# Two transformer-like blocks in one kernel: PSUM banks for intermediates, a different order of three openings, and attention 2 normalised at its output

## The chip, the cores and the metric

The kernel runs on one core of a Trainium2 chip. The metric is the device time of the whole kernel in microseconds (us). The engines work side by side and hand work over by semaphores: TensorE (PE) multiplies matrices into PSUM, VectorE (DVE) and ScalarE (ACT) compute elementwise and can read and write PSUM, GpSimd (POOL) computes elementwise on SBUF only, and SyncE (SP) issues the large transfers.

## The reference

The input is a sequence of 512 positions with 1024 channels, all in float32. The first block is run twice (two layers), the second block once.

```python
def first_block(x, ...):                         # two layers
    for l in range(2):
        h = rmsnorm(x, g_pre_mix[l])
        (c_q, c_kv, k_r, p_in, s_u, s_v, cv_b, cv_c, cv_x, gate_logits) = split_cols(h @ w_in[l])
        y_a = mla_branch(...) @ w_br_a[l]        # attention 1: 8 heads
        y_b = pool_branch(p_in, pool_w[l], pool_scale[l]) @ w_br_b[l]
        y_c = sgu_branch(s_u, s_v, ...) @ w_br_c[l]
        y_d = conv_branch(cv_b, cv_c, cv_x, ...) @ w_br_d[l]
        merged = sum(sigmoid(gate_logits)[b] * y for b, y in enumerate((y_a, y_b, y_c, y_d)))
        x = x + rmsnorm(merged @ w_out[l], g_post_mix[l])
        h = rmsnorm(x, g_pre_ffn[l])
        f = (silu(h @ w_ffn_gate[l]) * (h @ w_ffn_up[l])) @ w_ffn_down[l]
        x = x + rmsnorm(f, g_post_ffn[l])

def recurrent_block(x, ...):                     # the start of the second block
    gate, rec = split(x @ w_in)                  # 1024 channels each
    rec = causal_depthwise_conv(rec, conv_w, conv_b)           # 4 taps
    r, i = sigmoid(gates of rec)                 # 8 blocks of 128
    a = exp(-8 * r * softplus(-lam))
    h = scan(h = a * h + sqrt(1 - a * a) * (i * rec))          # along the sequence
    return (gelu(gate) * h) @ w_out

def second_block(x, ...):
    h = x + recurrent_block(rmsnorm_2(x, a_norm), ...)
    h = h + square(relu(rmsnorm_2(h, mlp_norm) @ w_up)) @ w_down
    k, v = shared_kv(h, ...)                     # keys normalised per head
    q = rmsnorm_2(rmsnorm_2(h, b_norm) @ w_q)
    p = softmax(q @ k.T * scale + bias)          # attention 2: 16 heads, chunk mask
    h = h + (p @ v) @ w_o
    return h + square(relu(rmsnorm_2(h, mlp_norm) @ w_up)) @ w_down
```

## The kernel before

Every tensor lies transposed: channels on the 128 partitions, the 512 positions along the row. X is 8 such tiles. A float32 product is made of three passes on rounded operands, `three` (matmuls at L831 to L833 for a whole unit): high part of the weights by high part of the data, high by low, low by high. The weights come in 476 **units** of 128 x 1024 words. A unit goes through four slots in SBUF: SyncE loads it (L309), ScalarE rounds it into the high part (`split_weights`, L370), GpSimd subtracts that into the low part in two halves (`low`, L340 and L342), TensorE multiplies it, 8 tiles by three passes, 24 products into one PSUM bank, and VectorE takes the bank. `tick(u)` on ScalarE splits unit u + 2. The data are split in the same way: a high part on ScalarE, a low part on VectorE (`x_lo` L1338, `lo_of` L1528).

Each engine has its instructions in an order written out by hand, and only semaphores tie them. Five places matter here.

- **The opening.** `norm` and `norm_tile` on ScalarE square a tile of X (L389) and make its high part (L391), tile by tile; VectorE (`norm_x`) adds the square to ACC (L1325) and makes the low part. TensorE runs the first unit tile by tile, then the sum of squares over the partitions (L901), then the second unit. ScalarE issues four small table loads before all that (L526).
- **The pool branch.** VectorE builds sums over windows of 2 to 16 positions from A (L1563 to L1574); TensorE multiplies them (L1088) right after unit 9 of the layer. Then come one unit, eight transposes for the gated branch (L1097), two units and its mixing (L1104). After the last input units and the value unit (L1119), attention 1 opens with scores (L1021).
- **The double norms**, four of them, where a block's output is normalised and added to X, and X at once normalised for the next block. VectorE copies or adds the last tile (L1373, L1657), ScalarE squares it and takes the root per position (L411), VectorE inverts it, ScalarE spreads it over 512 columns (RS2, L585), TensorE turns it (L913), and `post_norm` on VectorE scales, adds to X (L1357, L1358) and makes low parts. `together` on TensorE runs the first three units of the next block side by side, one tile of the data at a time, with a matmul for the sum of squares (L889) ahead of each tile.
- **The recurrent block.** ScalarE makes the first tap of the convolution (`tap`, L643), VectorE the other three (`conv`, L1692, L1693), TensorE the gates in four groups (`gates`), ScalarE sigmoids (L636, L637), tanh, exp, square and root, VectorE `gated`, `spread` (L1717), `recur` (L1723, L1724) and `product` (L1729). All intermediates are in SBUF. `together` starts the output units.
- **Attention 2**, 16 units of work of two heads and two blocks of queries. For each, TensorE computes scores (L946), VectorE adds the bias and takes maxima (`moved`, `maxima`, L1383 to L1392), ScalarE exponentiates (L440), VectorE inverts the sums (L1400), GpSimd scales the probabilities (L354), TensorE transposes them (L956), ScalarE copies them (L456 to L458), TensorE multiplies by the values (L969), ScalarE and VectorE split the output (L447, L1528).

## Time and profile before

| | us |
|---|---|
| median of 3 runs (2844.13 to 2852.17) | 2845.6 |
| the profiled execution | 2845.0 |
| its span | 2843.3 |
| TensorE busy in the span | 2737.2 (96%) |
| VectorE busy | 1229.2 (43%) |
| ScalarE busy | 1061.1 (37%) |
| GpSimd busy | 1340.3 (47%) |

The span is the time from the first to the last instruction in the profile; the execution's own time is 1.7 us longer. The busy shares are averages over the whole program. TensorE's mean granted clock was 0.982 of full speed; the profile knows two levels, 0.5 (1.2 GHz) and 1.0 (2.4 GHz). Matmul rows overlap, so the sum of their durations says more than the time they take one after the other.

### The profile page before, as it was taken

The numbers are of one execution on the slowest core, as the hardware profiler recorded it, in microseconds if no ns is written. First come the engines' busy times: TensorE is split into PE (matmuls) and PEld (weight loads), VectorE is DVE, ScalarE is ACT, GpSimd is POOL, SyncE is SP. The second block draws the span as 40 slices with busy tenths as digits, with TensorE's granted clock in tenths as the row PEclk, the third lists the DMA queues.
The fourth block names the chain that finished last, engine by engine and source line by source line (L and its number), as shares of the span: only waits on it lengthen the run. The fifth ranks groups of instructions, "written<-read, shape, count | busy, mean of one in ns | idle before, by whom it ended". The sixth has DMA issues, their size and how long they took to land.

```text
span 2843.3 us, 34289 instructions
## 1 busy us (share of the span) xinstructions
PE 2737.2 (96%) x12318; PEld 2213.5 (78%) x12318; DVE 1229.2 (43%) x1605; ACT 1061.1 (37%) x1566; POOL 1340.3 (47%) x1032
## 2 busy tenths in 40 slices
PE   8899999999999999999999999899999997899999
PEld 6688877888876888877888877688888885688887
DVE  5555555312246554455221268643224228453222
ACT  4244433322342344434222247433224347433222
POOL 4454543444453544453444445454444437454443
PEclk9999999999999999999999999999999998999999
DMA  3233332333332333322333322223333220123333
GB/s 132 82 97 97 104 87 69 97 97 98 98 100 74 104 95 98 97 89 74 97 97 96 97 89 82 81 90 97 98 97 126 80 88 8 52 91 98 97 99 97
DMA packets 72699, 259.15 MB, mean 91 GB/s; under 512 B 8192, under 2 KB 9088, under 8 KB 72448
## 3 DMA queue, kind: packets, MB, share of 16 engines
q1 hardware_dynamic: 71280, 254.17, 28.9%
q10 hardware_dynamic: 1296, 3.28, 0.3%
q8 instruction: 86, 1.41, 0.2%
q14 instruction: 37, 0.30, 0.0%
HBM read 255.31 MB, written 2.10 MB: 91 GB/s over the span
## 4 chain that ended last, share of the span: by engine, by line
issue 38%; PE 31%; POOL 26%; DVE 4%; ACT 1%; POOLq 0%; DVEq 0%
POOL w_lo L342 13%; POOL w_lo L340 12%; PE ps L831 9%; PE ps L833 9%; PE ps L832 9%; DVE XS L1808 1%; DVE fb L1807 1%; DVE st L1391 1%; POOL probs L354 1%; PE ps L1263 1%; PE ps L1265 1%; PE ps L1264 1%; ACT w_hi L370 0%; PE ps L1209 0%; ACT Y_hi L750 0%
## 5 line engine op out<-in xcount | busy, mean ns | idle before, releaser
L340 POOL TENSOR_TENSOR w_lo<-w_raw,w_hi 128x512 fp32r<-128x512 f32 x476 | 636.5, 1337 | 1466.0 <-ACT w_hi L370 1464.8
L831 PE MATMUL ps<-H_hi,w_hi 128*128 128x512 f32 x2240 | 901.8, 403 | 14.4 <-DVE H_lo L1338 13.8
L833 PE MATMUL ps<-H_hi,w_lo 128*128 128x512 f32 x2240 | 875.1, 391 | 0.0
L832 PE MATMUL ps<-H_lo,w_hi 128*128 128x512 f32 x2240 | 874.9, 391 | 0.0
L370 ACT ACTIVATE w_hi<-w_raw 128x1024 fp32r<-128x1024 f32 x476 | 500.0, 1054 | 583.9 <-DMA w_raw<-w_all 583.7
L342 POOL TENSOR_TENSOR w_lo<-w_raw,w_hi 128x512 fp32r<-128x512 f32 x476 | 654.4, 1375 | 0.0
L831 PEld LDWEIGHTS ps<-H_hi,w_hi 128*128 128x128 f32 x2240 | 422.8, 189 | 124.6 <-issue 24.9
L832 PEld LDWEIGHTS ps<-H_lo,w_hi 128*128 128x128 f32 x2240 | 422.9, 189 | 97.3 <-issue 12.5
L833 PEld LDWEIGHTS ps<-H_hi,w_lo 128*128 128x128 f32 x2240 | 422.1, 188 | 89.0
L831 PE MATMUL ps<-Y_hi,w_hi 128*128 128x512 f32 x1168 | 459.3, 393 | 19.5 <-POOL w_lo L342 11.5
L833 PE MATMUL ps<-Y_hi,w_lo 128*128 128x512 f32 x1168 | 456.5, 391 | 0.0
L832 PE MATMUL ps<-Y_lo,w_hi 128*128 128x512 f32 x1168 | 456.4, 391 | 0.0
L831 PEld LDWEIGHTS ps<-Y_hi,w_hi 128*128 128x128 f32 x1168 | 220.6, 189 | 67.4 <-POOL w_lo L342 12.4
L833 PEld LDWEIGHTS ps<-Y_hi,w_lo 128*128 128x128 f32 x1168 | 220.5, 189 | 46.6
L832 PEld LDWEIGHTS ps<-Y_lo,w_hi 128*128 128x128 f32 x1168 | 220.8, 189 | 45.3
L1807 DVE TENSOR_TENSOR fb<-fa,RS 128x512 f32<-128x512 f32 x64 | 63.4, 991 | 146.9 <-ACT fa L748 113.2
L1819 DVE TENSOR_TENSOR X<-X,ps 128x512 f32<-128x512 f32 x48 | 33.0, 688 | 207.5 <-PE ps L833 207.5
L1643 DVE TENSOR_TENSOR XS<-fb,ps 128x512 f32<-128x512 f32 x44 | 30.3, 688 | 194.7 <-PE ps L833 187.7
L606 ACT ACTIVATE Y_hi<-XS 128x512 fp32r<-128x512 f32 x44 | 27.8, 632 | 226.6 <-DVE XS L1645 226.6
L1454 DVE TENSOR_TENSOR G<-ps,RS 128x512 f32<-128x512 f32 x64 | 44.3, 692 | 135.0 <-PE ps L833 133.7
L474 ACT ACTIVATE G<-G 128x512 f32<-128x512 f32 x64 | 40.2, 631 | 157.3 <-DVE G L1454 157.3
L750 ACT ACTIVATE Y_hi<-XS 128x512 fp32r<-128x512 f32 x64 | 40.5, 632 | 141.2 <-DVE XS L1808 141.2
(240 smaller groups left out, 2513.0 us busy)
## 6 DMA issues: line engine op xcount, KB each, us to landing
w_raw<-w_all SPq DMA_DIRECT2D x476, 512.0 KB, 3.6
X<-xT SPq DMA_DIRECT2D x8, 256.0 KB, 6.5
rel_bias<-bias ACTq DMA_DIRECT2D x1, 2048.0 KB, 7.9
outT<-X SPq DMA_DIRECT2D x8, 256.0 KB, 3.4
sguw<-sgu_wT ACTq DMA_DIRECT2D x2, 256.0 KB, 4.4
sgub<-sgu_b ACTq DMA_DIRECT2D x2, 128.0 KB, 4.6
sgug<-sgu_g ACTq DMA_DIRECT2D x2, 128.0 KB, 5.1
CS<-cossin SPq DMA_DIRECT2D x1, 256.0 KB, 8.7
```

The source lines that it names most:

```text
L340: nc.gpsimd.tensor_tensor(w_lo[:, s, 0:UNIT // 2], w_raw[:, s, 0:UNIT // 2], f(w_hi[:, s, 0:UNIT // 2]), ALU.subtract).then_inc(w_lo_half, 1)
L342: nc.gpsimd.tensor_tensor(w_lo[:, s, UNIT // 2:UNIT], w_raw[:, s, UNIT // 2:UNIT], f(w_hi[:, s, UNIT // 2:UNIT]), ALU.subtract).then_inc(w ...
L370: nc.scalar.activation(w_hi[:, c % WSLOTS, :], w_raw[:, c % WSLOTS, :], ACT.Copy).then_inc(w_hi_ready, 1)
L474: nc.scalar.activation(dst, dst, ACT.Sigmoid).then_inc(sig_done, 1)
L750: nc.scalar.activation(Y_hi[:, j, :], XS[:, j % 2, :], ACT.Copy).then_inc(hi_ready, 1)
L831: MM(out, wh, xh, start=start, stop=False)
L832: MM(out, wh, xl, start=False, stop=False)
L833: return MM(out, wl, xh, start=False, stop=stop)
L1454: VE.tensor_tensor(dst, ps[:, bank(o), :], RS[:], ALU.mult).then_inc(g_lin, 1)
L1643: lk(VE.tensor_tensor(XS[:, j % 2, :], fb[:, j % 2, :], ps[:, (u0 + 2 * j + 1) % 4, :], ALU.mult))
L1807: lk(VE.tensor_tensor(fb[:, 0, :], fa[:, j % 2, :], RS[:], ALU.mult))
L1819: VE.tensor_tensor(X[:, m, :], X[:, m, :], ps[:, c % 4, :], ALU.add).then_inc(unit_out, 1)
```

## The change

- **Opening, layer 0.** ScalarE makes all eight high parts first, then the second unit's weights, then the squares; VectorE makes the eight low parts, then adds. TensorE runs units 0 and 1 before the sum of squares. The table loads of layer 0 are issued after the squares.
- **Pool branch, both layers.** The eight transposes and units 10 and 11 come ahead of the pool products; pool banks 4, 7, 7, 4. Input units 14 and 15 come ahead of the value unit, and the first scores wait for one unit less.
- **Double norms.** The last square of the mixing block is read from PSUM, ahead of the copy. The root's table is loaded by a dummy instruction. RS2 is no longer written: TensorE multiplies the 128 x 1 inverses, broadcast, by the identity. VectorE's second scaled tile comes between the add and the low part, ScalarE makes a tile's high part ahead of its square, and TensorE takes the sum of squares behind the tile's products. The merge before the first norm orders ScalarE's splits differently.
- **Recurrent block.** Taps 0 to 3, the squares, roots and drives of tiles 4 to 7 and all products go to PSUM banks 4 to 7. ScalarE's first sigmoids go ahead of tap 5, the split of the third output unit ahead of gelu 6. `together` begins the output units with two of them (`late=1`).
- **Attention 2.** GpSimd no longer scales the probabilities. TensorE turns the inverses with four more products per unit, ScalarE's third copy is 512 columns wide instead of 256, VectorE scales the output into XS, ScalarE makes its high part from there and GpSimd the low part.

```diff
-POOL_BANK = (4, 5, 6, 4)
-QK0, UV1 = 14, 16
+POOL_BANK = (4, 7, 7, 4)
+QK0, UV1 = 14, 17
+        def tapped(k):
+            return ps[:, 4 + k, :] if k < 4 else rec[:, k, :]
+        def spare(n):
+            return ps[:, 4 + n % 4, :]
+        def root_of(n):
+            return spare(n) if n >= 4 else lru_t[:, n, :]
...
             for h in range(H2):                                   # GpSimd, attention 2
-                g = 2 * H1 + h
-                eng.wait_ge(inv_ready, h + 1)
-                for n in range(4):
-                    o = kept(h, n // 2, n % 2)
-                    i = nc.gpsimd.tensor_scalar(o, o, st[:, g % 2, 12 + n:13 + n], None, ALU.mult)
-                i.then_inc(p_ready, 1)
+                eng.wait_ge(hi_ready, SPLIT["att2"] + h + 1)
+                nc.gpsimd.tensor_tensor(of_tiles(Y_lo, h // 2, h), scaled2(h), f(of_tiles(Y_hi, h // 2, h)), ALU.subtract).then_inc(lo_ready, 1)
...
                 if on_pe:                                         # ScalarE, norm_tile
+                    nc.scalar.activation(dst(k), src(k), ACT.Copy, scale=v(name, k)).then_inc(hi_ready, 1)
                     if k >= 2:
                         act.wait_ge(sq_summed, pb // 8 * 7 + k - 1)
...
-                    act.wait_ge(post_inv, p + 1)
-                    nc.scalar.activation(RS2[:].rearrange("p (j d) -> p j d", d=P), st[:, 0, 8:12, None].to_broadcast([P, 4, P]), ACT.Copy).then_inc(post_row, 1)
+                    nc.scalar.activation(hn[:, 0, 0:1], ones[:, 0:1], ACT.Sqrt)
...
+                    for k in range(DT):                           # ScalarE, opening
+                        act.wait_ge(x_loaded[k], 16)
+                        nc.scalar.activation(H_hi[:, k, :], X[:, k, :], ACT.Copy, scale=v("pre_mix0", k)).then_inc(hi_ready, 1)
+                    split_weights(1, 1)
...
+            gates(0)                                              # ScalarE, recurrent block
             tap(5)
-            gates(0)
...
+            tick(UAO)
             gelu(6)
-            tick(UAO)
...
                 for k in range(wide):                             # TensorE, together
                     tile(k)
-                    for u in range(u0, u0 + n):
+                    for u in range(u0, u0 + n - (1 if k < late else 0)):
+                        if late and k == late and u == u0 + n - 1:
+                            pe.wait_ge(w_lo_ready, u0 + n)
+                            for q in range(late):
+                                product(u, q)
                         product(u, k)
+                    if squares:
+                        squares(k)
...
-                pe.wait_ge(post_row, p + 1)                       # TensorE, post_norm
+                pe.wait_ge(post_inv, p + 1)
                 for j in range(4):
-                    m = nc.tensor.transpose(ps[:, 6, j * P:(j + 1) * P], RS2[:, j * P:(j + 1) * P], ident[:])
+                    m = MM(ps[:, 6, j * P:(j + 1) * P], st[:, 0, 8 + j:9 + j].to_broadcast([P, P]), ident[:], start=True, stop=True)
...
+                for s in (1, 0):                                  # TensorE, turn_pair
+                    for e in range(2):
+                        k = 12 + 2 * s + e
+                        m = MM(ps[64 * e:64 * e + 64, 6, (3 - s) * P:(4 - s) * P], st[:, u % 2, k:k + 1].to_broadcast([P, 64]), ident[:], start=True, stop=True)
...
-                    pe.wait_ge(p_ready, g + 1)
+                    pe.wait_ge(inv_ready, u + 1)
...
-                    lo_of("att2", h, of_tiles(Y_lo, h // 2, h), attended2, of_tiles(Y_hi, h // 2, h))   # VectorE
+                    VE.tensor_tensor(XS[:, h % 2, 0:2 * P], ps[:, 7, 0:2 * P], probsT2[:, h % 2, 10 * P:12 * P], ALU.mult).then_inc(scaled_done, 1)
```

On TensorE, around the pool branch of layer 0, the order before was this (SA and SB hold the window sums, A the input units' results, vnT the gated branch's normalised input):

```order
L831 MATMUL ps<-H_hi,w_hi 128x512 [waits unit_out,w_lo_ready]
...
L1088 MATMUL ps<-SA,poolw 64x512 [waits br_vec,layer_loaded]
L1088 MATMUL ps<-SB,poolw 64x512
...
L831 MATMUL ps<-H_hi,w_hi 128x512 [waits unit_out,w_lo_ready]
...
L1097 MATMUL ps<-ident,A 128x128 [waits unit_out,lo_ready]
L1097 MATMUL ps<-ident,A 128x128 x7
...
L1104 MATMUL ps<-sguw,vnT 64x128 [waits br_vec]
```

and now it is this:

```order
L1112 MATMUL ps<-ident,A 128x128 [waits unit_out]
L1112 MATMUL ps<-ident,A 128x128 x7
L844 MATMUL ps<-H_hi,w_hi 128x512 [waits unit_out,w_lo_ready]
...
L1121 MATMUL ps<-SA,poolw 64x512 [waits std_ready,br_vec,layer_loaded]
L1121 MATMUL ps<-SB,poolw 64x512 x2
L1121 MATMUL ps<-SA,poolw 64x512
...
L1128 MATMUL ps<-sguw,vnT 64x128 [waits br_vec]
```

The pool products moved behind the transposes and two units (48 products).

On ScalarE, in the recurrent block, from the split of the unit B2 + 8 on, the order before was this (Y_hi is a high part, rec the convolution, lru_r and lru_i the sigmoids):

```order
L626 ACTIVATE Y_hi<-rec 128x512 [waits src_ready] x2
L643 ACTIVATE rec<-recp,V 128x512 [waits unit_out]
L636 ACT_TABLE_LOAD
L636 ACTIVATE lru_r<-ps,V 128x512 [waits lru_mm]
L637 ACTIVATE lru_i<-ps,V 128x512
...
L370 ACTIVATE w_hi<-w_raw 128x1024 [waits w_loaded3]
```

and now it is this:

```order
L641 ACTIVATE Y_hi<-rec 128x512 [waits src_ready] x2
L651 ACT_TABLE_LOAD
L651 ACTIVATE lru_r<-ps,V 128x512 [waits lru_mm]
L652 ACTIVATE lru_i<-ps,V 128x512
...
L658 ACTIVATE rec<-recp,V 128x512 [waits unit_out]
L379 ACTIVATE w_hi<-w_raw 128x1024 [waits w_loaded3]
```

The tap of tile 5 moved behind the first four sigmoids.

On TensorE, one unit of attention 2 before (probs are the probabilities, probsT their transposes):

```order
L946 MATMUL ps<-K_59,Q_58 128x384 [waits s_free]
L946 MATMUL ps<-K_59,Q_58 128x384
L946 MATMUL ps<-K_59,Q_58 128x256 x2
L956 MATMUL ps<-ident,probs_55 128x128 [waits pt_a,p_ready]
L956 MATMUL ps<-ident,probs_55 128x128 x9
L969 MATMUL ps<-probsT_56,V_87 64x256 [waits lo_ready,pt_a]
```

and now:

```order
L965 MATMUL ps<-K_59,Q_58 128x384 [waits s_free]
L965 MATMUL ps<-K_59,Q_58 128x384
L965 MATMUL ps<-K_59,Q_58 128x256 x2
L975 MATMUL ps<-ident,probs_55 128x128 [waits pt_a,inv_ready]
L975 MATMUL ps<-ident,probs_55 128x128 x9
L980 MATMUL ps<-ident,st 64x128 x4
L992 MATMUL ps<-probsT_56,V_87 64x256 [waits scaled_done,pt_a]
```

The transposes wait for VectorE's inverse (inv_ready) and no longer for GpSimd (p_ready), and four products are new.

## Rows read from the trace of the kernel before

**Rows 1.** The page, part 1: busy us (share of the span) xinstructions
```profile
PE 2737.2 (96%) x12318; PEld 2213.5 (78%) x12318; DVE 1229.2 (43%) x1605; ACT 1061.1 (37%) x1566; POOL 1340.3 (47%) x1032
```

**Rows 2.** Waits of TensorE: who waited for whom, us in total, times, longest
```profile
PE ps L956 <- POOL probs L354: 14.6, 12, 2.9
PE ps L1088 <- DVEq L1576: 14.0, 2, 7.0
PE ps L831 <- DVE H_lo L1338: 13.8, 5, 10.9
PE ps L831 <- POOL w_lo L342: 11.5, 2, 10.8
PE ps L889 <- ACT SQ L385: 9.5, 4, 2.4
PE ps L909 <- DVE ACC L1325: 9.2, 4, 2.3
...
PE ps L913 <- ACT RS L585: 6.4, 4, 1.6
PE ps L831 <- issue: 5.8, 2, 5.5
```

**Rows 3.** Five stretches: length, busy PE PEld DVE ACT POOL, PE's clock, DMA share, GB/s
```profile
76.50:87.60 11.10, 4.08 (x10) 1.28 (x10) 8.23 (x12) 0.32 (x1) 0.71 (x1) 0.69 0.16 47
1726.00:1733.00 7.00, 5.39 (x13) 4.26 (x14) 6.00 (x8) 3.78 (x6) 3.33 (x2) 0.51 0.00 0
1790.90:1804.50 13.60, 5.60 (x13) 4.43 (x14) 12.44 (x16) 5.41 (x10) 3.39 (x2) 0.50 0.02 7
2364.30:2428.60 64.30, 51.62 (x395) 35.65 (x394) 56.29 (x103) 50.75 (x156) 59.85 (x56) 0.92 0.00 1
2428.60:2445.50 16.90, 12.75 (x86) 8.98 (x87) 1.60 (x5) 6.94 (x20) 8.54 (x8) 0.72 0.00 1
```

**Rows 4.** The opening in order of time: start us, us, instruction, idle before
```profile
10.94 0.77 PE L831 MATMUL ps<-H_hi,w_hi 128*128 128x512 f32 x1 [10.94 <-DVE H_lo L1338]
...
13.07 0.75 DVE L1338 SCALAR_TENSOR_TENSOR H_lo<-X,V,H_hi 128x512 fp32r<-128x512 f32 x1
...
20.63 1.64 DVE L1338 SCALAR_TENSOR_TENSOR H_lo<-X,V,H_hi 128x512 fp32r<-128x512 f32 x1
...
24.32 1.41 PE L831 MATMUL ps<-H_hi,w_hi 128*128 128x512 f32 x1
```

**Rows 5.** The first pool product of layer 0, in order of time
```profile
83.56 1.08 PE L1088 MATMUL ps<-SA,poolw 64*64 64x512 f32 x1 [7.02 <-DVEq L1576]
```

**Rows 6.** The double norm after layer 0's mixing block, in order of time
```profile
456.67 0.69 DVE L1373 COPY Dn<-ps 128x512 f32<-128x512 f32 x1 [3.18 <-PE ps L833]
...
460.86 0.63 ACT L585 ACTIVATE RS<-st 128x512 f32<-128x512 f32 x1 [0.31 <-DVE st L1353]
...
466.60 0.92 PE L831 MATMUL ps<-H_hi,w_hi 128*128 128x512 f32 x1
```

**Rows 7.** Groups of VectorE from 1696 to 1788: busy us, mean ns, idle before
```profile
L1692 DVE SCALAR_TENSOR_TENSOR rec<-recp,V,rec 128x512 f32<-128x512 f32 x16 | 17.8, 1111 | 1.8 <-ACT rec L643 1.3
L1717 DVE SCALAR_TENSOR_TENSOR lru_t<-lru_u,lru_t 128x512 f32<-128x512 f32 x8 | 9.8, 1226 | 0.4
```

**Rows 8.** The recurrent block's output units, in order of time
```profile
1794.34 1.04 ACT L370 ACTIVATE w_hi<-w_raw 128x1024 fp32r<-128x1024 f32 x1
...
1798.90 0.79 PE L831 MATMUL ps<-Y_hi,w_hi 128*128 128x512 f32 x1 [10.84 <-POOL w_lo L342]
```

**Rows 9.** Groups of attention 2, 2364.3 to 2428.6
```profile
L354 POOL TENSOR_SCALAR probs<-probs,st 128x384 f32<-128x384 f32 (+3 forms) x52 | 55.5, 1089 | 5.0 <-DVE st L1400 5.0
```

**Rows 10.** Attention 2, first copies of three of VectorE's units, in order of time
```profile
2364.29 0.42 DVE L1383 COPY probs<-ps 128x256 f32<-128x256 f32 x1 [0.63 <-PE ps L946]
...
2395.71 0.42 DVE L1383 COPY probs<-ps 128x256 f32<-128x256 f32 x1 [0.95 <-PE ps L946]
...
2424.18 0.42 DVE L1383 COPY probs<-ps 128x256 f32<-128x256 f32 x1
```

More of the change, by code:

```diff
@@ L848, in unit, with together @@
                 m.then_inc(w_used, 1)
-            def together(u0, n, xh, xl, ready, squares, wide=5):
-                pe.wait_ge(w_lo_ready, u0 + n)
+            def together(u0, n, xh, xl, ready, squares, wide=5, late=0):
+                pe.wait_ge(w_lo_ready, u0 + n - (1 if late else 0))
                 pe.wait_ge(unit_out, u0 + n - 4)
@@ L870, in together @@
                         m = product(u, k)
+                        if u == u0 and squares:
+                            squares(k)
                     m.then_inc(w_used, 1)
@@ L1082, in _ @@
                 gemm(w0 + 7, 3, Hh, Hl)
-                pe.wait_ge(layer_loaded, 64 * (l + 1))
-                pe.wait_ge(br_vec, 3 * l + 1)
-                for g in range(4):
-                    r = slice(64 * (g % 2), 64 * (g % 2) + 64)
-                    m = MM(ps[r, POOL_BANK[g], :], poolw[r, g // 2, :], (SA, SB)[g % 2][r, g // 2, 16:528], start=True, stop=True)
-                m.then_inc(br_mm, 1)
-                gemm(w0 + 10, 1, Hh, Hl)
-                pe.wait_ge(lo_ready, SPLIT[f"pool{l}"] + 2)
                 pe.wait_ge(unit_out, w0 + 8)
@@ L1098, in _ @@
                 m.then_inc(br_mm, 1)
-                gemm(w0 + 11, 2, Hh, Hl)
+                gemm(w0 + 10, 2, Hh, Hl)
+                pe.wait_ge(layer_loaded, 64 * (l + 1))
+                pe.wait_ge(br_vec, 3 * l + 1)
+                pe.wait_ge(std_ready, NORMS[f"ckv{l}"][0] + 1)
+                for g in (0, 1, 3, 2):
+                    r = slice(64 * (g % 2), 64 * (g % 2) + 64)
+                    m = MM(ps[r, POOL_BANK[g], :], poolw[r, g // 2, :], (SA, SB)[g % 2][r, g // 2, 16:528], start=True, stop=True)
+                m.then_inc(br_mm, 1)
+                gemm(w0 + 12, 1, Hh, Hl)
                 pe.wait_ge(br_vec, 3 * l + 3)
@@ L1183, in _ @@
                 gelu_unit(n)
-            together(UAO, 3, Yh, Yl, SPLIT["lru"], None)
+            together(UAO, 3, Yh, Yl, SPLIT["lru"], None, late=1)
             gemm(UAO + 3, DT - 3, Yh, Yl)
@@ L1345, in norm_x @@
                 for k in range(DT):
+                    x_lo(split, name, k)
+                for k in range(DT):
                     add_squares(name, k)
-                    x_lo(split, name, k)
                 link(root(name, RS[:]))
@@ L1581, in _ @@
                 dve.wait_ge(br_vec, 3 * l + 2)
+                take(10)
+                dve.wait_ge(a_chain, 5 * l + 5)
+                link(VE.reciprocal(st[:, 0, 12:16], st[:, 1, 8:12]))
+                for n in range(4):
+                    i = VE.scalar_tensor_tensor(vnT[:, n, :], ps[:, 5 + n // 2, (n % 2) * 256:(n % 2) * 256 + 256], st[:, 0, 12 + n:13 + n],
+                                                sgug[:], ALU.mult, ALU.mult)
+                    if n < 3:
+                        link(i)
+                i.then_inc(br_vec, 1)
+                dve.wait_ge(br_vec, 3 * l + 3)
+                take(11)
                 for t in range(2):
@@ L1615, in _ @@
                 project(l, w0 + QK0, N_PART * l + 1, 0)
-                take(14)
+                take(14, 15)
                 dve.wait_ge(w_used, w0 + UV1 + 1)
@@ L1621, in _ @@
                     freed(i_ == 3)
-                take(15)
                 for h in range(H1):
@@ L1625, in _ @@
                 attended(l)
-                for k in range(U_OUT):
+                for k in range(U_OUT - 1):
                     copy_out(U["out"] + k, Dn[:, k, :])
```

166 lines of the change are left out of this document (83 added, 83 removed).

## The prediction

> **What bounds the kernel now.** I read the page first, then the waits of TensorE, then seven stretches of the busy-time table, and only then rows in order of time. TensorE is busy 96% of the 2843.3 us span [rows 1]. So nothing that merely shortens work on ScalarE, VectorE or GpSimd counts; what counts is the time in which TensorE waits, and the time after a wait in which its products run at half clock. The list of its waits is short: the eight largest sum to 14.6 + 14.0 + 13.8 + 11.5 + 9.5 + 9.2 + 6.4 + 5.8 = 84.8 us, of which 10.9 is the start of the program [rows 2, 4]. The second loss is the clock. From 1790.9 to 1804.5 the granted clock is 0.50 (1.2 GHz of 2.4), and 13 products take 5.60 us, 0.43 each; at full clock that is 0.215, and a unit of 24 products about 5.3 us [rows 3]. So each microsecond of products at half clock loses half of itself. The change touches the place behind each of the eight waits. The sum is made against the profiled execution's 2845.0 us (span plus 1.7 around it); the median of the runs is 0.6 above it.
>
> **Opening.** Before, ScalarE squares and splits each tile of X in turn and VectorE adds a square between two low parts, so the first unit is fed one tile per 1.5 us: it starts at 10.94 and the second unit at 24.32 [rows 4]. That is 13.4 us for one unit and one sum. After, the eight high parts come first, one per 0.6 us, the squares behind them, and four table loads leave the head of ScalarE's queue. With TensorE at half clock for its first 12 products (5.2 us) and then at full clock (2.7), the unit takes 8 us from a start that is up to 1 us earlier. What hides the squares is the second unit (5.3 us), which now runs ahead of the sum. Eight adds at 0.7 to 1.0 us need 5.6 to 8, so I leave 1.3 us for a late sum. Gain 7 (bounds 4.5 and 9, the latter with no wait for the sum). A low part that runs beside GpSimd costs 1.64 us [rows 4], and the second unit's weights are now split beside the low parts; that is in the lower bound.
>
> **Pool branch and first attention slot.** The branch's four products wait 7.02 us for VectorE's window sums, once per layer: the 14.0 of [rows 2, 5]. After, TensorE first does the gate branch's eight transposes and two units (0.6 + 10.6 us), whose inputs were taken long before, and comes to the pool products at about 88 where the sums end at 83.5 [rows 5]. So 4.5 us of slack cover them, also if GpSimd's splitting slows the last sums. Gain 14.0. In the stretch after the wait the clock averages 0.69 [rows 3]; about 4 us of products at half clock there and 2.8 in the second layer give back 3.4. The value unit, moved behind the last input unit, lets the first scores wait for a unit whose copy is long done; that wait is 0.8 per layer, outside the eight. VectorE's four value copies then come ahead of the first maxima, under 16 us of gate products. Gain 19 (bounds 14 and 20).
>
> **The four double norms.** From the last product to the first of the next block there are 10.0 us: the copy that follows the last product begins at 456.67, ScalarE writes the row from 460.86 (0.63), products resume at 466.60 [rows 6]. After a mixing block the last square reads PSUM (-0.7), the weight split is moved ahead, the ScalarE hop of 0.63 with its two hand-overs goes (-0.9), and the high part comes before the square and the second add after the first low part (-0.7 each): 7.6. After an FFN the first saving is absent: 8.3. But the first sum of squares, some 0.9 us, was hidden in the old wait and now stands among the products, and products that begin sooner find the clock still low for longer. Net 0.6 per norm, 2.5 in all (bounds -3 and 8). The merge before the first norm, where the order of ScalarE's splits changes, I take at 1.5 (bounds -1 and 4).
>
> **Recurrent block.** Three waits: 0.7, 5.5 ("issue") and 10.8 (the 11.5 and 5.8 of [rows 2]). What stands behind them is VectorE. Its three-operand steps on SBUF average 1.11 us in the convolutions and 1.23 in the spreads [rows 7]; one beside an idle GpSimd takes 0.75, one beside a busy one 1.64 [rows 4]. An operand in PSUM leaves that conflict: four convolutions (12 steps), four spreads and four drives, 20 steps at 0.36 to 0.48 saved, 8 us on VectorE's chain. In the first part this brings the fourth and fifth convolution forward by some 5 us. ScalarE then does the first sigmoids ahead of tap 5, so that TensorE's second gate group no longer waits: 5.5 and 0.7 go, and of the 5.39 us of products at clock 0.51 [rows 3] half, 2.7; these 8.9 are not added, since the output unit below is where they count. What is late next is ScalarE: its second sigmoids stand behind tap 6, which waits for VectorE, and come about 5.5 us earlier, not 9; the fourth gate group then waits some 3.8 us where it waited 0.3. The large wait ends with the low half of the third output unit's weights, split at 1794.34 [rows 8] behind gelu 6. Now it is ahead of gelu 6, and two units begin with their first tile without it. Everything there follows the chain, 5.5 us earlier and shorter by the PSUM steps: I get the first output tile at about 1782 and the last of the 72 products at about 1800, where before it was at 1817 (start 1798.90 [rows 8], 72 x 0.215 = 15.5 of products, 2.8 of them twice for half clock [rows 3]). That is 17; 1.5 off for a new low stretch of clock behind the 3.8. Gain 15.5 (bounds 6, where the fourth group and the output unit wait as long as before less the order gain, and 20).
>
> The Trainium skill ("VectorE: DVE Perf Modes", the errata section) gives VectorE an operand from PSUM a larger fixed cost than one from SBUF, 120 cycles against 58. At its 0.96 GHz that is 0.065 us a step, and by the page 20 steps would lose 1.3 us. The trace does not bear it out: the SBUF step alone takes 0.75 [rows 4], the PSUM copy 0.69 [rows 6] (different operations, so only the nearest pair). The skill's "SBUF — State Buffer" (who interferes with whom) says that a VectorE step with two SBUF inputs and a GpSimd step block each other for the whole instruction. By that a contended step should cost up to its own 0.75 plus GpSimd's 1.3; the row shows 1.64 [rows 4], so the gain a step would be 1.3 by the rule and is 0.9 by the row.
>
> **Attention 2.** GpSimd scales the probabilities, 1.09 us a step and four a unit [rows 9], before TensorE may transpose them: 14.6 us of waits [rows 2]. After, transposes wait only for VectorE's reciprocal; the row is turned with four small products, and VectorE scales the 256 output columns. Where does the bound go? VectorE is busy 56.29 of 64.3 us [rows 3] and back to back between the two weight splits on GpSimd. Twelve units take 59.9 us, from 2364.29 to 2424.18, 4.99 each [rows 10]; the one that starts at 2395.71 waits for TensorE, which waits for GpSimd behind a weight split. Without those the units run at 4.5, and that is VectorE's own work, since scaling 256 columns out of PSUM takes what the low part took (0.42 by the copy of that size [rows 10]). So the steady part gains only 12 x 0.5 = 6. TensorE's busy 51.62 us [rows 3] are 4.0 a unit, partly at half clock; four more products at 0.13 (51.62 over 395) make 4.5, some 4.2 at full clock, against 4.5: close, and hidden while the clock is full. ScalarE's wider third copy adds 0.2 to 3.8. At the end the last three units are paced by GpSimd's 4.3 before, 16.9 us for 86 products at clock 0.72 [rows 3]; after, by transposes, copies and values, about 3.4. That is 4.5 more. GpSimd's low parts (0.7) hide behind the output unit's first seven tiles. Gain 9.5 of 10.5, for hand-overs (bounds 3 and 12).
>
> **Sum.** 7 + 19 + 2.5 + 1.5 + 15.5 + 9.5 = 55; 2845.0 - 55 = 2790.0, and about 2790 as a median too.
>
> **Rivals.**
> (a) Only the order gains come through. The recurrent chain through ScalarE holds TensorE up as before at the fourth gate group and the output unit (gain 6, not 15.5), or attention 2 gives 3 because VectorE, TensorE and ScalarE all stand within 0.5 us of the period: 2845 - 55 + 9.5 = 2799.5, or 2796.5; both, 2806. For it: VectorE is busy 88% of attention's body, and the last four convolutions stay in SBUF. Against: the low-part wait named GpSimd, whose place in the order has changed.
> (b) More comes: the opening's sum is in time, the norms' clock recovers at the same distance, the output unit is fed without a stall: 7 + 2 + 5 + 4.5 more, some 10 to 15 of it together, 2776 to 2780.
> (c) Waits only change place (the change does not do what it says): each moved wait reappears at the next hand-over, within 0.3%. Against it: the 7 us of the pool wait have two units with inputs long ready to fill them.
> (d) Slower: TensorE in attention 2 stays at 1.2 GHz. A unit there would cost it twice 4.2 = 8.4 us in place of 4.99, over 16 units 55 us lost in place of 9.5 gained: 2845 - 45.5 + 55 = 2854.5. It decides once products at half clock (8.4) outlast VectorE's period (4.5), so that TensorE never idles but never is granted full clock. For it: clock 0.72 in the tail and 0.92 in the body [rows 3]; against it: the body's clock rises in the stretches with fewer waits.
>
> **Chances.** Forecast (2784 to 2796) 0.50; (a) 0.29; (b) 0.15; (c) 0.02; (d) 0.02; 0.02 for something unseen. The likeliest is 2790. The range takes in (b) but for its end and (a) with both parts: 2775 to 2808, which leaves out about 2 in 10. 0.3% (8.5 us) is about what a measurement of this kernel can tell from no change: faster 0.95, same 0.025, slower 0.025.
>
> **What would show it.** No wait for the pool products, in either layer. Second unit at about 18 and the first sum after it. About 7.6 and 8.3 us between last and first product at the norms. No 5.5 us wait at the second gate group, a new one of some 4 at the fourth, and output units beginning near 1800 less what is gained before. In attention 2, copies 4.5 us apart throughout and a tail of about 12 us. Mean clock above the present one. It is wrong if TensorE's waits still sum to over 60 us, if VectorE's steps with PSUM operands take more than 0.8, or if the clock in attention 2 is below 0.85.

## The result and the profile after

| us | before | changed |
|---|---|---|
| median | 2848.9 (2844.1 to 2853.1, 4 runs) | 2808.7 (2807.1 to 2810.4, 4 runs) |
| the profiled execution's span | 2843.3 | 2808.7 |

The ratio is 0.9859 with a 95% interval of 0.9839 to 0.9880: the change makes the kernel 1.2 to 1.6% faster, 34 to 46 us. The forecast was 2790 with a range of 2775 to 2808. The direction was right, the gain too large, and the time lies just outside the range. Over all comparisons below the kernel before took 2840.9 to 2855.2; its profiled execution was one of the short ones (median 2851.7 in 17 runs), so against it the gain is smaller: 2843.3 - 2808.7 = 34.6 us of span where 55 were forecast. By medians it is 40.2 of 55. The forecast took 55 off the short execution's 2845.0; about 4 us of the 19 by which 2790 was missed are that base, and the other 15 are the terms.

Part 1 of the page of the changed kernel answers to [rows 1]. GpSimd has 48 instructions and 61 us less, TensorE 144 records more and 1.2 us less:

```profile
PE 2736.0 (97%) x12462; PEld 2220.7 (79%) x12462; DVE 1224.8 (44%) x1605; ACT 1064.9 (38%) x1566; POOL 1279.6 (46%) x984
```

These are its waits of TensorE, to be read beside [rows 2] (who waited for whom, us in total, times, longest):

```profile
PE ps L844 <- POOL w_lo L355: 17.6, 4, 10.7
PE ps L844 <- DVE H_lo L1361: 13.9, 5, 3.3
PE ps L928 <- DVE ACC L1348: 11.5, 4, 4.3
PE ps L975 <- ACT probsT L468: 7.2, 9, 1.5
PE ps L965 <- DVE probs L1411: 5.1, 3, 2.4
PE ps L844 <- issue: 3.5, 2, 3.3
PE ps L844 <- DVE M_lo L1540: 3.2, 2, 1.8
PE ps L932 <- DVE st L1377: 2.5, 4, 0.6
```

The two lines that the pool branch and GpSimd's scaling had are gone (14.0 and 14.6), and so are the 9.5 and 6.4 of the norms. But the wait for ACC, VectorE's sum of squares, has grown from 9.2 to 11.5 us, with 4.3 as its longest where it was 2.3, and waits for H_lo, in the norms, stand where the square was. Low parts of weights are now waited for four times: 10.7 at the start of the program, 1.2 twice and 4.4. In attention 2 the longest row is now for ScalarE's copies of the transposes, 7.2. The eight lines add up to 64.5 us, where the forecast had named over 60 as a sign that it was wrong.

To see where the time went, the same products are looked up in both traces; the difference of their starts (of their ends in the rows on a last product and on the end of the products) is the gain so far.

| place | before | changed | gain so far | the part | forecast |
|---|---|---|---|---|---|
| second sum of squares of layer 0 | 47.41 | 43.25 | 4.2 | opening 4.2 | 7 |
| first input product behind slot 1, layer 0 | 155.36 | 142.52 | 12.8 | pool, slot 8.7 | 9.5 |
| last product of the first mixing block | 456.57 | 444.15 | 12.4 | merge -0.4 | 1.5 |
| first product of w_ffn_down | 561.56 | 549.86 | 11.7 | norm 1: -0.7 | 0.6 |
| second sum of squares of layer 1 (norm 2 lies between) | 878.11 | 871.39 | 6.7 | norm 2: -5.0 | 0.6 |
| first input product behind slot 1, layer 1 | 985.50 | 970.69 | 14.8 | pool, slot 8.1 | 9.5 |
| last product of the second mixing block | 1285.44 | 1270.40 | 15.0 | merge 0.2 | - |
| first product of w_ffn_down | 1390.72 | 1375.50 | 15.2 | norm 3: 0.2 | 0.6 |
| end of the products before the first gates | 1712.95 | 1700.05 | 12.9 | norm 4: -2.3 | 0.6 |
| first product of the square-relu block | 1845.18 | 1820.67 | 24.5 | recurrent 11.6 | 15.5 |
| output unit of attention 2 | 2445.50 | 2411.21 | 34.3 | attention 2: 9.8 | 9.5 |

The four double norms lose 7.8 us where the forecast had them gain 2.5. That is half of the missing 20; the recurrent block (3.9), the opening (2.8) and the pool part (2.2) have most of the rest.

This is the second double norm in the trace of the changed kernel, in order of time (start us, us, instruction, idle before):

```profile
821.67 1.06 ACT L379 ACTIVATE w_hi<-w_raw 128x1024 fp32r<-128x1024 f32 x1 [2.25 <-DMA w_raw<-w_all]
...
822.81 1.26 POOL L353 TENSOR_TENSOR w_lo<-w_raw,w_hi 128x512 fp32r<-128x512 f32 x1 [0.93 <-ACT w_hi L379]
822.87 0.63 ACT L399 ACTIVATE SQ<-Dn 128x512 f32<-128x512 f32 x1
822.87 3.42 DVE L1348 TENSOR_TENSOR ACC<-ACC,SQ 128x512 f32<-128x512 f32 x2
...
824.03 1.71 POOL L355 TENSOR_TENSOR w_lo<-w_raw,w_hi 128x512 fp32r<-128x512 f32 x1
...
826.34 1.81 PE L928 MATMUL ps<-ones,ACC 128*128 128x1 f32 x8 [4.30 <-DVE ACC L1348]
...
828.78 2.07 PE L932 MATMUL ps<-ident,st 128*128 128x128 f32 x8 [0.64 <-DVE st L1377]
...
834.19 0.76 PE L844 MATMUL ps<-H_hi,w_hi 128*128 128x512 f32 x1 [3.34 <-DVE H_lo L1361]
```

The weight split, moved ahead of the last square, ends at 822.7. GpSimd then subtracts from 822.81 to 825.74, beside VectorE's last two additions of squares, which take 3.42 us together (822.87 to 826.29); 1.42 is what the same two take undisturbed (below). The sum over the partitions starts 4.3 us behind the last product in place of 2.3. By then the clock has fallen: it is 0.5 from about 826 to 840, so the sum takes 1.81 in place of 1.05. The turn is 8 records and 2.07 us; with the row of before it was 4 records and 1.12, also at half clock. The first product comes 12.15 us behind the last one, where [rows 6] gave 10.0 and the forecast 8.3.

The recurrent block, VectorE's steps in groups from 1682 to 1774 (busy us, mean ns, idle before), to be read beside [rows 7]:

```profile
L1725 DVE SCALAR_TENSOR_TENSOR rec<-recp,V,rec 128x512 f32<-128x512 f32 x8 | 9.1, 1131 | 6.3 <-ACT rec L658 6.0
L1725 DVE SCALAR_TENSOR_TENSOR ps<-recp,V,ps 128x512 f32<-128x512 f32 x8 | 6.0, 756 | 0.3
...
L1750 DVE SCALAR_TENSOR_TENSOR lru_t<-ps,lru_t 128x512 f32<-128x512 f32 x4 | 2.8, 692 | 0.2
```

and the two long waits of TensorE there, with the GpSimd step that ends the first, the VectorE step just ahead of the end of the second and, from the output units, what corresponds to [rows 8]:

```profile
1717.15 0.67 ACT L651 ACTIVATE lru_r<-ps,V 128x512 f32<-128x512 f32 x1
...
1720.25 2.00 ACT L379 ACTIVATE w_hi<-w_raw 128x1024 fp32r<-128x1024 f32 x2
...
1725.52 1.26 POOL L355 TENSOR_TENSOR w_lo<-w_raw,w_hi 128x512 fp32r<-128x512 f32 x1
...
1726.84 0.50 PE L844 MATMUL ps<-Y_hi,w_hi 128*128 128x512 f32 x1 [4.38 <-POOL w_lo L355]
...
1774.69 0.69 DVE L1735 TENSOR_TENSOR gelu_g<-ps,RS 128x512 f32<-128x512 f32 x1
...
1775.54 0.77 PE L844 MATMUL ps<-Y_hi,w_hi 128*128 128x512 f32 x1 [3.27 <-issue]
```

With an operand in PSUM a step takes 0.69 to 0.76, also where GpSimd runs beside it. The steps in SBUF average 1.13: 0.75 alone and up to 1.84 beside GpSimd. That part is as forecast. The wait of 5.51 at the second group is 0.20, the 0.70 is gone and the 10.84 is 3.27: the output units start when VectorE has taken the gelu unit 6 out of its bank (L1735). But a wait of 4.38 has come at the third group of gates.

Attention 2 (columns as in [rows 3]): the first row is 13 units, the second the tail.

```profile
2340.00:2398.20 58.20, 53.21 (x498) 38.68 (x497) 53.80 (x102) 52.70 (x154) 13.02 (x15) 0.98 0.00 1
2398.20:2411.20 13.00, 10.09 (x110) 8.05 (x110) 1.91 (x6) 8.34 (x21) 2.91 (x4) 1.00 0.01 3
```

A unit takes 4.5 us (58.2 / 13), as forecast, and the tail 13.0, where the forecast had about 12. TensorE, VectorE and ScalarE are now busy within 1.1 us of each other, 53.21, 53.80 and 52.70.

### The profile page after: what moved, and what is told of

Same layout as the page of the kernel before. It is cut to its first block, busy times and chain, and to the rows that moved or that the text cites. A ratio compares the mean times of both kernels' runs of the same rounds, so it can differ in the third digit from the quotient of the medians.

```text
span 2808.7 us, 34501 instructions
## 1 busy us (share of the span) xinstructions
PE 2736.0 (97%) x12462; PEld 2220.7 (79%) x12462; DVE 1224.8 (44%) x1605; ACT 1064.9 (38%) x1566; POOL 1279.6 (46%) x984
## 4 chain that ended last, share of the span: by engine, by line
issue 37%; PE 33%; POOL 24%; DVE 3%; ACT 2%; POOLq 0%; DVEq 0%
POOL w_lo L355 12%; POOL w_lo L353 12%; PE ps L844 10%; PE ps L846 10%; PE ps L845 10%; DVE XS L1845 1%; DVE fb L1844 1%; ACT w_hi L379 1%; DVE st L1417 1%; PE ps L1286 1%; PE ps L1288 1%; PE ps L1287 1%; PE ps L1232 0%; ACT Y_hi L763 0%; PE ps L975 0%
## 5 line engine op out<-in xcount | busy, mean ns | idle before, releaser
L484 ACT ACTIVATE G<-G 128x512 f32<-128x512 f32 x64 | 40.2, 632 | 161.2 <-DVE G L1485 161.2
```

The costliest lines, as they stand in the source:

```text
L484: nc.scalar.activation(dst, dst, ACT.Sigmoid).then_inc(sig_done, 1)
```

## The experiments

Each gives the median of its own runs and the ratio to the kernel before with its 95% interval. The comparison with the changed kernel's 2808.7 (ratio 0.9859, 0.9839 to 0.9880) is one of medians of 4 or 5 runs, taken at different times. Of the variants of the changed kernel only `pool_order_as_before` and `all_repairs` have a ratio clear of that interval (`transpose_and_split` touches it). Smaller differences rest on the times themselves and on the aligned traces. The times of the changed kernel are 2807.1 to 2810.4; those of `recurrent_order_as_before` and `opening_as_before` overlap with them.

### The double norms

**norms_as_before** puts the old norms into the changed kernel:

```diff
-                tick(U["ffn"])
-                norm_tile(f"post_mix{l}", lambda k: ps[:, (U["out"] + k) % 4, :], (w_used, U["out"]), DT - 1, None, None)
-                post_root(f"post_mix{l}")
+                post_square(f"post_mix{l}", U["out"], DT - 1)
+                post_root(2 * l, f"post_mix{l}", U["ffn"])
...
```

> The changed kernel with its four double norms put back to the order of before (row written by ScalarE and transposed, weight split behind the last square, square ahead of the high part, sum of squares ahead of a tile's products); everything else stays changed. Theory: the double norms are the step that failed. Aligned by the same units, the changed kernel loses 0.5, 5.0, 0.6 and 2.3 us at its four norms, 8.4 in all, so this kernel takes 2808.7 - 8.4 = about 2800. Rival 1, the forecast's sum: the new norms gain 2.5, so this one takes 2811. Rival 2: the loss is only the clock falling at another moment in one execution, then it is within 2 us of 2808.7.

2804.9, ratio 0.9837 (0.9823 to 0.9850). The distances from last to first product are 10.0, 10.5, 10.0 and 10.0, against 9.6, 12.2, 8.6 and 10.4. The changed kernel is slower with its new norms, by 3.8 us of median. That is half of what the theory gave: up to the first gates this kernel is 5.6 us ahead of the changed one in the traces, and then loses 1.2 in the recurrent block, where its clock is low for 3.4 us more.

**only_double_norms** is the kernel before with the new norms and nothing else.

> The kernel before with the new double norms alone; nothing else is changed. Theory: the four norms are slower by themselves and not through the rest of the change: the last-to-first distance is 10.7 us and more behind a mixing block and 11 to 12 behind a feed-forward block, against 10.0, and this kernel is 4 (the median difference of the run with the norms of before) to 8 us (the aligned traces) slower than before: 2849 to 2853 where before's profiled execution had 2845.0, ratio 1.001 to 1.003. Rival 1, the forecast's sum: 2.5 faster, ratio 0.999. Rival 2: the loss is the meeting of these norms with the new order of the merge ahead of them, then the distance is 8 to 9 us here and the ratio 0.998.

2855.5 in 12 runs, against 2851.7 for the kernel before in 17, ratio 1.0015 (1.0004 to 1.0026): 4 us slower, by itself. Its second norm:

```profile
837.79 1.31 PE L912 MATMUL ps<-ones,ACC 128*128 128x1 f32 x8 [3.25 <-DVE ACC L1328]
839.74 2.07 PE L916 MATMUL ps<-ident,st 128*128 128x128 f32 x8 [0.64 <-DVE st L1356]
845.15 0.76 PE L832 MATMUL ps<-H_hi,w_hi 128*128 128x512 f32 x1 [3.34 <-DVE H_lo L1341]
```

The distance is 10.6 here, and 10.1, 9.7 and 10.4 at the others. Rival 1, the forecast's term, has fallen, and so has rival 2. The theory's distances, 10.7 and more behind a mixing block, were too long; the loss of 4 us held.

**split_behind_square** moves the split back and hides the table load:

```diff
-                tick((l + 1) * U_LAYER)
+                nc.scalar.activation(hn[:, 0, 0:1], ones[:, 0:1], ACT.Sqrt)
                 post_square(f"post_ffn{l}", U["ffn"] + U_FFN - DT, DT - 1)
+                tick((l + 1) * U_LAYER)
                 post_root(f"post_ffn{l}")
```

(with the same order behind the mixing blocks, and the load taken out of `post_root`; the two moves were not tried apart).

> The changed kernel, with one edit: at the four double norms ScalarE loads the root's table ahead of the last square, and splits the next block's first weights behind that square, not ahead of it. Theory: GpSimd's subtraction of these weights ran beside VectorE's last two additions of squares and made one or both take 1.7 us in place of 0.69; without it TensorE's wait for the sum falls from 4.30 and 3.25 (behind the two feed-forward blocks) to about 2.3, and from 2.50 to about 1.5 behind the first mixing block: 4 us, and some 0.5 to 1.5 more where the clock no longer falls ahead of the sum: 2803 to 2804.5. Rival: the subtraction then runs beside VectorE's first additions to X, which have two operands in SBUF, and costs there what it saved: 2808.

2804.2, ratio 0.9833 (0.9819 to 0.9846). Its second norm:

```profile
822.51 1.42 DVE L1349 TENSOR_TENSOR ACC<-ACC,SQ 128x512 f32<-128x512 f32 x2
...
823.99 1.05 PE L929 MATMUL ps<-ones,ACC 128*128 128x1 f32 x8 [2.31 <-DVE ACC L1349]
824.17 1.26 POOL L353 TENSOR_TENSOR w_lo<-w_raw,w_hi 128x512 fp32r<-128x512 f32 x1 [2.65 <-ACT w_hi L379]
...
825.68 1.16 PE L933 MATMUL ps<-ident,st 128*128 128x128 f32 x8 [0.64 <-DVE st L1378]
```

GpSimd starts after the additions, which take 1.42 us, and the wait is 2.31. The clock is still full when the turn comes, and the same 8 records take 1.16 us, not 2.07 (1.16 at the fourth norm too, 1.78 and 1.67 behind the mixing blocks). So the contended additions cost 2.0 us, and here they pushed the sum and the turn into a low stretch of the clock that begins at about the same time in both traces (826.4 and 826.8). A longer wait isn't needed for that: in `all_repairs`, with the same wait of 2.31 at the second norm, the clock falls at 821.4 and the sum takes 1.87 us. All four distances are 8.2 to 8.5. The rival is refuted: the subtraction ends at 826.65, before the first addition to X.

**turn_by_transpose**:

```diff
-                    m = MM(ps[:, 6, j * P:(j + 1) * P], st[:, 0, 8 + j:9 + j].to_broadcast([P, P]), ident[:], start=True, stop=True)
+                    m = nc.tensor.transpose(ps[:, 6, j * P:(j + 1) * P], st[:, 0, 8 + j:9 + j].to_broadcast([P, P]), ident[:])
```

> The changed kernel, with one edit: the four products that turn the inverses are issued as transposes of the broadcast column in place of ordinary float32 products. Theory: an ordinary float32 product is done in two passes (8 records, 2.07 us from first to last) and a transpose in one (4 records, 1.12 us as before the change), so each norm is 0.95 shorter: 3.8 in all, about 2805. Rival: the 2.07 us are due to the broadcast operand or to the half clock there, then the transposes of the broadcast take 2 us as well and the time stays at 2808.7.

2803.0, ratio 0.9831 (0.9818 to 0.9845); by medians 5.7 less, in the traces 3.8. Its second norm again:

```profile
825.05 1.05 PE L928 MATMUL ps<-ones,ACC 128*128 128x1 f32 x8 [3.25 <-DVE ACC L1348]
826.74 0.91 PE L932 MATMUL ps<-ident,st 128*128 128x128 f32 x4 [0.64 <-DVE st L1377]
```

A transpose of the broadcast column leaves 4 records and takes 0.65 to 1.12 us, by the clock. The two passes are real, but the rival was not all wrong: half clock makes the other half of the 2.07.

**transpose_and_split** has both edits.

> Both edits together: transposes of the broadcast column, and the weight split behind the last square with the table load ahead of it. Theory: the two are one behind the other on the same chain, so they add: 3.8 + 4 to 5 = some 8, about 2800, with some 9 us from last to first product at each norm where the changed kernel has 10.7 to 12.2. It would then equal the kernel with the norms of before or beat it by what the row and the order of the high part save. Rival: the shorter chain meets the low part of the weights on GpSimd, which becomes the last to be ready: 2804.

2801.6, ratio 0.9825 (0.9812 to 0.9839), 7.1 less than the changed kernel and 3.3 less than with the old norms. The distances are 7.6, 8.0, 7.9 and 8.0: the forecast's 7.6 and 8.3. So the forecast had described this kernel and not the one that it was given.

```profile
823.40 1.05 PE L929 MATMUL ps<-ones,ACC 128*128 128x1 f32 x8 [2.31 <-DVE ACC L1349]
825.09 0.65 PE L933 MATMUL ps<-ident,st 128*128 128x128 f32 x4 [0.64 <-DVE st L1378]
829.08 0.77 PE L845 MATMUL ps<-H_hi,w_hi 128*128 128x512 f32 x1 [3.33 <-DVE H_lo L1362]
```

Measured to the start of the 60th product behind the norm, where the sum of squares among the products counts as well, the four norms add up to 124.1 us before, 132.0 changed, and 122.0 here: 2.1 better than before. The other traces tell how typical that is. The changed kernel's norms stand in eight kernels: 126.6 to 134.7, 130.5 on average. The old norms stand in two, the kernel before and `norms_as_before`: 124.1 and 125.1. So the new norms cost about 6 us, and the changed kernel's trace shows more than its share. With the split moved back alone they take 124.2, with transposes alone 126.6.

### The recurrent block

**recurrent_without_psum** (`tapped(k)` is rec, `spare` and `root_of` go back to the tiles in SBUF):

```diff
-                nc.scalar.activation(tapped(k), recp[:, k, 3:515], ACT.Identity, bias=v("a_conv_b", k), scale=v("a_conv", 24 + k)).then_inc(rec_tap, 1)
+                nc.scalar.activation(rec[:, k, :], recp[:, k, 3:515], ACT.Identity, bias=v("a_conv_b", k), scale=v("a_conv", 24 + k)).then_inc(rec_tap, 1)
...
```

> The changed kernel with taps, squares, roots, drives and products of the recurrent block back in SBUF; the new order of ScalarE and the late third output unit stay. Theory: the whole block was worth 11.6 us; VectorE's chain is longer by about 8 us of contended steps, and of that about 5.6 come through to TensorE, because the order alone is worth 6: 2814.3. Rival: the chain that holds TensorE up runs through ScalarE and the weights' low parts on GpSimd, so the banks of PSUM give nothing: 2809.

2816.1, ratio 0.9879 (0.9860 to 0.9897): the banks are worth 7.4 us, 6.9 in the aligned traces. TensorE waits 4.6 us at the second group, 2.4 at the third and 5.9 at the output units, 12.9 in place of 7.9:

```profile
1713.34 0.77 PE L846 MATMUL ps<-Y_hi,w_hi 128*128 128x512 f32 x1 [4.61 <-issue]
1731.60 0.80 PE L846 MATMUL ps<-Y_hi,w_hi 128*128 128x512 f32 x1 [2.42 <-POOL w_lo L355]
```

**recurrent_order_as_before**:

```diff
-            gates(0)
             tap(5)
+            gates(0)
...
-            tick(UAO)
             gelu(6)
+            tick(UAO)
...
-            together(UAO, 3, Yh, Yl, SPLIT["lru"], None, late=1)
+            together(UAO, 3, Yh, Yl, SPLIT["lru"], None)
```

> The changed kernel with ScalarE's old order in the recurrent block (tap 5 ahead of the first sigmoids, the split of the third output unit behind gelu 6) and the output units begun with three; the intermediates stay in PSUM. Theory: the 5.5 us wait at the second group of gates comes back, less what the shorter chain saves, and the third output unit is late again: 5 to 6 us lost, 2814. The wait of 4.4 us at the third group, which the changed kernel has and the kernel before has not, shrinks to under 1 because TensorE comes there later. Rival: what the order gives at the second group it loses at the third, and only the late third unit counts: 2811.

2811.8, ratio 0.9862 (0.9843 to 0.9881): 3.1 us (2.2 in the aligned traces), nearer to the rival's 2811 than to 2814, though the times (2808.1 to 2814.3) overlap with the changed kernel's. The waits at the gates are these:

```profile
1710.74 0.47 PE L844 MATMUL ps<-Y_hi,w_hi 128*128 128x512 f32 x1 [1.10 <-issue]
1724.92 0.50 PE L844 MATMUL ps<-Y_hi,w_hi 128*128 128x512 f32 x1 [0.30 <-POOL w_lo L355]
1734.12 0.47 PE L844 MATMUL ps<-Y_hi,w_hi 128*128 128x512 f32 x1 [0.70 <-issue]
```

With PSUM in place the second group waits only 1.10 in the old order, and the third 0.30. So the banks took away the 5.5, and the new order of the sigmoids saves 0.9 more at the cost of 4.1. What the old order loses is at the output units, 8.19 against 3.27.

**gate_order_as_before** tells the two apart: of the diff above only tap 5 is moved back.

> The changed kernel with one edit: tap 5 again ahead of ScalarE's first four sigmoids; PSUM banks, the early split of the third output unit and the late third unit stay. Theory: the sigmoids first save TensorE 1.1 us at the second group of gates and cost it 4.4 at the third, where the low part of the third group's weights is late on GpSimd. So this kernel is 3.3 faster at the start of the third group, and the output units, which wait for VectorE's chain, keep a part of it: 2808.7 - 1 to 3.3 = 2805.4 to 2807.7. Rival: VectorE's chain sets the output units alone, then all of it is given back there: 2808.7.

2803.6, ratio 0.9837 (0.9819 to 0.9855): 5.1 less by medians. In the traces this kernel is 3.8 us further ahead behind the block than in front of it (9.3 against 5.5); the waits are 1.09, 0.30, 0.75 and 3.23. All of the gain reaches the output units, so the rival has fallen; the gain is somewhat above the theory's 1 to 3.3. Against `recurrent_order_as_before`, the early split and the late third unit are worth 6.0 us in the traces and 8.2 by medians.

### The other parts

**attention2_as_before** (GpSimd scales, no turned inverses, VectorE makes the low part).

> The changed kernel with attention 2 put back: GpSimd scales the probabilities, no row is turned, VectorE makes the low part of the output. Theory: the part is worth what it was worth in the two traces aligned by the same products, 34.3 - 24.5 = 9.8 us (forecast 9.5), so this kernel takes 2808.7 + 9.8 = 2818.5. Rival: it is worth 3 (VectorE, TensorE and ScalarE all near the period), 2812.

2815.3, ratio 0.9883 (0.9862 to 0.9904): 6.6 us by medians, between the rival's 3 and the theory's 9.8. The two traces with and without this part alone, the same otherwise, differ by 7.6 over attention 2. TensorE waits 15.3 us for GpSimd's probabilities again.

**pool_order_as_before** (pool products right behind unit 9, value unit ahead of the last input unit).

> The changed kernel with the pool branch, the value unit and the first scores in the order of before. Theory: the part is worth what the aligned traces give, 8.7 us in layer 0 and 8.1 in layer 1, so 16.8 are lost: 2825.5. That is net of a wait of 1.2 us per layer for a weight's low part behind the first slot of attention 1, which the forecast did not have and which should be gone here. Rival: 7.0 per layer for the wait alone, 2822.7, if the clock gives nothing back.

2825.8, ratio 0.9911 (0.9885 to 0.9937): 17.1 us. The waits of 7.0 for the window sums and of 0.78 for the first scores are back, and the low part behind slot 1, for which the changed kernel waits here, is not waited for:

```profile
142.52 0.47 PE L844 MATMUL ps<-H_hi,w_hi 128*128 128x512 f32 x1 [1.23 <-POOL w_lo L355]
```

**opening_as_before** (a tile's square, high part and addition in turn, the sum behind the first unit).

> The changed kernel with layer 0's opening as before (tiles squared and split in turn, sum of squares behind the first unit, table loads first). Theory: the part is worth 4.2 us, as the start of the third unit shows in the aligned traces, and not the 7 of the forecast, which left the second unit and the sum out on one side: 2813. Rival: 7 us as forecast, 2815.7.

2812.2, ratio 0.9861 (0.9843 to 0.9878): 3.5 us by medians, 3.7 in the traces where the openings end. Some of its times (2809.6 to 2814.6) are not above the changed kernel's highest, so the traces carry this reading. The changed opening's two turning points are

```profile
10.69 0.76 PE L844 MATMUL ps<-H_hi,w_hi 128*128 128x512 f32 x1 [10.69 <-POOL w_lo L355]
...
25.93 1.13 PE L920 MATMUL ps<-ACC,ones 128*128 128x512 f32 x2 [1.60 <-DVE ACC L1348]
```

### A faster version

**all_repairs** has the two edits of the norms, the old gate order, and

```diff
+            gelu_out(6)
             recur(6)
             product(2)
             recur(7)
-            gelu_out(6)
```

> The changed kernel with four edits: the two of the double norms (transposes of the broadcast column; table load, last square, weight split in this order), the old gate order, and VectorE taking the gelu unit 6 out of its bank ahead of the sixth recurrence, since the output units' first tile waited 3.3 us for that bank in the changed kernel. Theory: 2801.6 as measured with the two edits of the norms, less 1 to 3.3 for the gates and 1 to 3 for the bank: 2796 to 2799. Rival: the output units are paced by VectorE's chain from the second tile on, so that an earlier start only spreads the wait over the tiles: 2800 to 2801.6.

2794.8 (2794.5 to 2800.2), ratio 0.9807 (0.9790 to 0.9823): 14 us below the changed kernel's median, just under the theory's 2796 to 2799, and the fastest here. Of it the first tile's bank gave little: the output units start at 1760.65, and then wait 2.2 us for the third unit's low part,

```profile
1765.97 0.49 PE L845 MATMUL ps<-Y_hi,w_hi 128*128 128x512 f32 x1 [2.23 <-POOL w_lo L355]
```

so the wait was mostly moved (behind the block it is 4.5 us further ahead than in front of it, and 3.8 of that came with the gate order).

## Why the prediction was wrong

**The double norms are the step that failed**: "Net 0.6 per norm, 2.5 in all (bounds -3 and 8)". Measured alone they cost 4 us by medians, and 7.8 in the aligned traces (about 6 on average over the traces), below the lower bound. Two things were left out. "The weight split is moved ahead" was counted as free; its other half on GpSimd lands beside VectorE's additions and costs 2.0, 1.0 and 1.0 us at three of the norms. That is the same 1.64 against 0.75 on which the forecast built its gain in the recurrent block [rows 4]; it was used where an operand leaves SBUF and not where a GpSimd step moves. The turn by "broadcast, by the identity" was priced like the transposes that it replaces, but runs in 8 records for 4. Each costs more where it meets a low stretch of the clock: at the second norm the sum takes 1.81 in place of 1.05 and the turn 2.07 in place of 1.16. What was forecast of the last square, the hop and the order of high part and second add came true as a sum, and was not tried one by one: with the two omissions mended the distances are 7.6 to 8.0 and the four norms gain 2.1, where 2.5 were forecast.

**Recurrent block, 15.5 forecast, 11.6 measured.** The price of the PSUM steps was right (0.69 to 0.76), and the banks alone are worth 7.4. A new wait of "some 3.8" was forecast at the fourth group, for ScalarE's second sigmoids; it is 4.38 at the third, for the low part of its weights, which ScalarE splits only behind those sigmoids. As forecast, the wait at the output units no longer ends with the third unit's low part; but 3.3 us stayed for a bank that VectorE had not emptied. The credit of 5.5 for the order at the second group was wrong in kind. With the banks and the old order that wait is 1.1, with the new order and no banks 4.6, and with both 0.2; so most of it belongs to the banks, and the reordering is a net loss.

**Opening, 7 forecast, 4.2 and 3.5 measured**, below its lower bound of 4.5. The mechanism was right (no wait for the sum but 1.6, second unit at 18.7 where about 18 was forecast). The size was not: with the forecast's own figures for the new opening, 10.0 + 8 + 5.3 + 1.3 + 0.9 = 25.5 for the third unit, and a third unit of before that starts at 31.1, the gain is 5.6. Measured there it is 4.6 (26.5). The start came only 0.25 earlier and not 1, as GpSimd's low part of the first unit ends last.

**Pool and first slot, 19 forecast, 16.8 and 17.1 measured.** No wait for the pool products, as forecast. What is missing is the 1.2 us per layer behind slot 1.

**Attention 2, 9.5 forecast, 9.8 in the aligned traces of before and changed.** With this part alone undone it is 7.6 in the traces and 6.6 by medians; the unit's 4.5 us came as forecast, and the clock of the body is 0.98. Rival (d) did not occur.

**The merge, 1.5 forecast**, gives nothing: -0.4 and 0.2. It was not tried by itself.

The sum had one slip in its reading of the waits. Its "eight largest" leave out TensorE's wait in attention 2 for VectorE to add the bias and empty the scores' banks, 7.4 us (L946 on L1385), which is larger than the 6.4 and the 5.8 that it has. All of TensorE's waits together were 102.9 us before and are 69.5 now. No term of the sum hangs on this.

The terms of the trace miss the sum by 20; the medians, 40.2 of 55, by 15. The parts' medians and aligned traces differ by up to 4 us (norms 3.8 and 7.8, attention 6.6 and 9.8), and a part of that is drift between executions. The kernel with the old gate order was already 5.5 us ahead of the changed one at the first gates, where the two have the same instructions. The low stretches of the clock lie at other moments in each, for example an added 3.4 us between 1224 and 1230 in four of the kernels. What sets those moments stays open. So a term of less than 3 us can't be read from one pair of traces here.

## What to carry to other kernels

When an instruction moves, follow what it feeds: a weight split that costs ScalarE nothing has a second half on another engine, and the price is paid by whoever shares SBUF with it. Price an operation that replaces another by its records, not by its result: a float32 product with the identity is not a transpose. Where two edits both aim at one wait, ask what each is worth when the other is in: here the banks alone had taken the wait for which the order was changed.

## What the runs showed of the hardware

- A 128x128 float32 product by the identity gives 2 records where a transpose of the same broadcast column gives 1: four of them take 1.16 us against 0.65 at full clock, 2.07 against 1.12 at half clock.
- Steps of VectorE with one operand in PSUM and one in SBUF take 0.69 to 0.76 us each beside a busy GpSimd, and two additions from SBUF 3.42 us beside it against 1.42 without. PSUM as the output alone doesn't free a step: products of two operands in SBUF that write to PSUM (L1763) take 0.88 to 1.12 beside GpSimd and 0.70 alone.
- The granted clock can fall within a double norm, and its moment isn't tied to the length of TensorE's wait. With a wait of 2.31 us at the second norm the sum over the partitions takes 1.05 us in `transpose_and_split` and 1.87 in `all_repairs`, where the clock was already 0.5.
